# The first expert's rows by counted ranks, and the selection for all experts beside its products

## What is computed

```python
def _ec_moe(h, w_router, w_gate, w_up, w_down):
    Bn, T, _ = h.shape
    cap = EC_CAPACITY_FACTOR * T // N_EXPERTS
    probs = jax.nn.softmax((h @ w_router).astype(jnp.float32), axis=-1)
    gates, idx = lax.top_k(jnp.swapaxes(probs, 1, 2), cap)
    bidx = jnp.arange(Bn)[:, None, None]
    xs = h[bidx, idx]
    a = jax.nn.silu(jnp.einsum('becd,edf->becf', xs, w_gate)) * jnp.einsum('becd,edf->becf', xs, w_up)
    y = jnp.einsum('becf,efd->becd', a, w_down) * gates[..., None].astype(h.dtype)
    return jnp.zeros_like(h).at[bidx, idx].add(y)

# in the layer:   x = x + gate1 * mixer(...);  h = rmsnorm(x) * (1 + scale2) + shift2
#                 x = x + gate2 * _ec_moe(h, ...)
# latent and context tokens each choose within their own set; the order of an expert's rows does not matter
```

## Time and profile before

| | |
|---|---|
| median of 3 runs | 855.3 us (855.23 to 855.87) |
| profiled execution | 855.45 us |
| its span | 853.7 us |
| PE busy | 831.0 us, 97% of the span |
| DVE busy | 493.0 us, 58% |
| ACT busy | 236.8 us, 28% |
| POOL busy | 63.1 us, 7% |
| granted TensorE clock, mean | 0.995 |
| DMA | 275.34 MB, mean 323 GB/s |

### The profile page before, as it was taken

How to read it: one execution, slowest core, us unless ns; L and a number is a source line. 1 busy time by engine, 2 the same in 40 slices (tenths; PEclk the granted TensorE clock), 3 DMA queues, 4 the chain that set the end, 5 groups by cost and what they waited for, 6 DMA issues and landing times.

```text
span 853.7 us, 14512 instructions
## 1 busy us (share of the span) xinstructions
PE 831.0 (97%) x6037; PEld 456.5 (53%) x6037; DVE 493.0 (58%) x1197; ACT 236.8 (28%) x466; POOL 63.1 (7%) x73
## 2 busy tenths in 40 slices
PE   6999999999999998999999999999999999999995
PEld 5798899899898876333333333333333333333322
DVE  3576552859366566576546556456456456465436
ACT  5557544544243335020110110111111011011005
POOL 1000000000000003110010011011011011010033
PEclk9999999999999999999999999999999999999998
DMA  9955625352319938999999999999999999999984
GB/s 329 301 203 189 223 82 197 113 197 78 133 31 344 369 126 319 416 408 428 411 411 428 412 410 430 412 408 429 412 412 422 416 412 419 419 412 412 427 340 161
DMA packets 51045, 275.34 MB, mean 323 GB/s; under 512 B 5226, under 2 KB 14542, under 8 KB 38820
## 3 DMA queue, kind: packets, MB, share of 16 engines
q1 hardware_dynamic: 45484, 255.68, 74.4%
q0 software_dynamic: 3968, 13.83, 5.5%
q10 hardware_dynamic: 1528, 4.90, 1.5%
HBM read 260.90 MB, written 13.57 MB: 321 GB/s over the span
## 4 chain that ended last, share of the span: by engine, by line
PE 88%; DMA 3%; DVE 3%; ACT 2%; SPq 1%; issue 1%; POOL 0%; POOLq 0%; DVEq 0%; ACTq 0%
PE pair L2365 25%; PE pair L1975 16%; PE pair L2387 13%; PE pair L2337 13%; PE pair L2396 7%; PE pair L2212 6%; PE pair L1915 2%; PE pair L2010 2%; DMA scale_b<-in_w_mod 2%; DMA p1w<-in_w_mod 1%; DMA xs<-hn,first_ctx 1%; PE pair L2123 1%; PE pair L1924 1%; PE pair L2145 0%; PE pair L2141 0%
## 5 line engine op out<-in xcount | busy, mean ns | idle before, releaser
L2365 PE MATMUL pair<-ring,xT 128*64 128x512 f32 x1024 | 224.1, 594 | 0.9 <-ACT xT L1124 0.9
L2365 PEld LDWEIGHTS pair<-ring,xT 128*64 128x64 f32 x1024 | 71.9, 137 | 142.9 <-issue 142.3
L2387 PE MATMUL pair<-ring,aT 128*64 128x512 f32 x512 | 113.4, 595 | 0.6 <-DVE aT L1754 0.6
L2337 PE MATMUL pair<-ring,xT 128*32 128x512 f32 x1024 | 113.4, 594 | 0.0
L1132 ACT ACTIVATE xT<-xT,mod,scale 128x64 f32<-128x64 f32 x120 | 41.4, 427 | 217.0 <-DVE xT L1754 201.4
L1754 DVE STREAM_TRANSPOSE xT<-xs 32x256 f32<-32x256 f32 x180 | 78.3, 435 | 3.0
L1754 DVE STREAM_TRANSPOSE aT<-act_l 32x128 f32<-32x128 f32 x256 | 77.5, 303 | 4.1
L2387 PEld LDWEIGHTS pair<-ring,aT 128*64 128x64 f32 x512 | 35.8, 137 | 77.6 <-issue 76.8
L1975 PE MATMUL pair<-hT_hi,w_hi 128*128 128x320 f32 x320 | 76.0, 319 | 0.0
L2337 PEld LDWEIGHTS pair<-ring,xT 128*32 128x32 f32 x1024 | 31.5, 110 | 80.2 <-issue 80.2
L1975 PE MATMUL pair<-hT_lo,w_hi 128*128 128x320 f32 x320 | 73.1, 310 | 0.0
(11 more groups left out here) (305 smaller groups left out, 937.3 us busy)
## 6 DMA issues: line engine op xcount, KB each, us to landing
ring<-in_w_up SPq DMA_DIRECT2D x32, 2048.0 KB, 29.0
ring<-in_w_down SPq DMA_DIRECT2D x32, 2048.0 KB, 18.8
ring<-in_w_gate SPq DMA_DIRECT2D x31, 2048.0 KB, 24.6
p1w<-in_w_mod SPq DMA_DIRECT2D x8, 2048.0 KB, 8.7
p1w<-in_w_in SPq DMA_DIRECT2D x5, 2048.0 KB, 8.0
p1w<-in_w_mod SPq DMA_DIRECT2D x7, 1024.0 KB, 11.4
x_sb<-in_x_sample SPq DMA_DIRECT2D x8, 512.0 KB, 5.7
p1w<-in_w_out SPq DMA_DIRECT2D x2, 2048.0 KB, 8.6
```

What stands on the lines that cost most here:

```text
L2337: ins = mm(ctx_ps[32 * g:32 * g + 32, :], xt[:, 4 * half + j, CAP_L:96], w[:, j, n * 512:(n + 1) * 512], start=half == 0 and j == 0, stop= ...
L2365: ins = mm(ps[64 * n:64 * n + 64, :], xt[:, kk, 0:CAP_L], w[:, j, n * 512:(n + 1) * 512], start=kk == 0, stop=kk == KC - 1)
L2387: ins = mm(y_ps[0][r:r + 64, :], aT[:, j, 64 * fh:64 * fh + 64], wd[:, j, n * 512:(n + 1) * 512], start=fh == 0 and j == 0, stop=fh == 1 a ...
```

## The change

Expert 0's latent rows no longer come from the eight rounds. TensorE spreads expert 0's probabilities of the 512 latent tokens over all partitions (`eR`). For each token VectorE counts how many others have a larger probability (equal ones count if they come earlier), which is its rank (`first_ranks`); a comparison with 0 to 63 gives a one-hot matrix (`first_hot`). TensorE multiplies it with the token numbers and the probabilities (`sel`, `selg`, `choose_first`, in the middle of the context tile's projection), which gives the 64 indices and gains. The eight rounds, the context tile's residual, norm and router, and the context choice are then cut up and stand between one another on VectorE; on TensorE the context router, `pTc`, `ixTc`, `ixT`, the second row of `g2` and `pcT` lie within or behind expert 0's latent products. One half of the context residual moves from ScalarE and GpSimd to VectorE (`ctx_high`), the copy of the context router's parts and the scaled context rows move from ScalarE to VectorE. The fillers are gone. Block 6 of the weights is issued ahead of the wait for `ctx_scaled`.

```diff
             sp.wait_ge(xs_full[0], 16)
+            load_rows(6)
             sp.wait_ge(ctx_scaled, 1)
             sp.dma_start(hn[tile(NT - 1), :], xr[:, 0, :]).then_inc(hn_out[0], 16)
-            load_rows(6)
...
+            pool.wait_ge(job_done, job("lg2") + 1)
+            g.iota(probs_t[:, :, E:E + 1], pattern=[[P, NT], [0, 1]], base=0, channel_multiplier=1,
+                   allow_small_or_imprecise_dtypes=True)
+            g.iota(places[:, :], pattern=[[1, CAP_L]], base=0, channel_multiplier=0, allow_small_or_imprecise_dtypes=True)
+            link(g.memset(lower[:, :], 1.0))
+            g.affine_select(out=lower[:, :], in_=lower[:, :], compare_op=ALU.is_ge, fill=0.0, base=-1,
+                            pattern=[[-1, P]], channel_multiplier=1).then_inc(pad_ready, 1)
...
             gather_first()
+            pool.wait_ge(idx_ready, 4)
             gather(1)
-            pool.wait_ge(idx_ready, 3)
+            pool.wait_ge(idx_ready, 5)
...
+            first_tokens(0, 2)
+            h2_turn(NT - 1)
+            act.wait_ge(x2c_ready, 2)
+            square_sum(NT - 1)
+            first_tokens(2, KC)
+            act.wait_ge(smax_ready, 2)
+            a.activation(probs[:, NT - 1, :], probs[:, NT - 1, :], ACT.Exp).then_inc(exp_ready, 1)
...
+                for t in range(NT - 1):
+                    ins = v.scalar_tensor_tensor(out=compared[4][:, tile(t)], in0=row[:, tile(t)], scalar=probs[:, t, 0:1],
+                                                 in1=lower[:, :], op0=ALU.is_equal, op1=ALU.mult, accum_out=ranks[:, 0, t:t + 1])
+                link(ins)
+                for t in range(1, NT - 1):
+                    ins = v.tensor_scalar(early[t], row[:, 0:P * t], probs[:, t, 0:1], ranks[:, 0, t:t + 1],
+                                          ALU.is_ge, ALU.add, accum_out=ranks[:, 1, t:t + 1])
+                link(ins)
+                for t in range(NT - 1):
+                    link(v.tensor_scalar(late[t], row[:, P * t:T_LAT], probs[:, t, 0:1],
+                                         ranks[:, 1 if t else 0, t:t + 1], ALU.is_gt, ALU.add, accum_out=ranks[:, 2, t:t + 1]))
+                    v.tensor_scalar(first_hot[:, t, :], places[:, :], ranks[:, 2, t:t + 1], None, ALU.is_equal).then_inc(selr_ready, 1)
...
             softmax(0, NT - 1, 1)
-            largest(probs_half[:, :], CAP_L, topv_l, topi_l)
+            normalise(NT - 2)
+            first_ranks()
+            turned_probs()
+            first_chosen()
+            rounds(0, 2)
+            ctx_high()
+            v.memset(xT[:, 0, :, SLOTS:96], 0.0).then_inc(pads_zero, 1)
+            rounds(2, 3)
+            high_chunks(NT - 1)
+            rounds(3, 4)
+            ctx_parts()
+            ctx_normal()
+            router_row(NT - 1)
+            softmax(NT - 1, NT, 2)
+            rounds(4, 5)
+            ctx_largest()
+            rounds(5, 6)
+            pp = result(dve, "ixTc")
+            v.tensor_copy(first_ctx[:, :], pp[0:CAP_C, E:2 * E][:, 0:1]).then_inc(idx_ready, 1)
+            rounds(6, 8)
             merge_halves()
...
                 if k == 0:
+                    choice()
+                    dve.wait_ge(g2_ready, 2)
                     tokens(e + 1, k + 1)
...
+            def first_row():
+                pe.wait_ge(probs_ready, 1)
+                pp = claim(pe, "eR")
+                for t in range(NT - 1):
+                    ins = turn(pp[:, tile(t)], probs[:, t, 0:1].to_broadcast([P, P]), ident[:, :])
+                end(ins, "eR")
+
+            def choose_first():
+                pe.wait_ge(selr_ready, NT - 1)
+                pp = claim(pe, "sel")
+                for half in range(2):
+                    for t in range(NT - 1):
+                        ins = mm(pp[CAP_L * half:CAP_L * half + CAP_L, 0:2], first_hot[:, t, :], probs_t[:, t, 0:E + 1:E],
+                                 start=t == 0, stop=t == NT - 2)
+                    end(ins, ("sel", "selg")[half])
+
+            first_row()
             turn_probs("pT", 1, range(NT - 1))
...
-            output_projection(4, 1)
+            output_projection(4, 1, range(3))
+            choose_first()
+            output_projection(4, 1, range(3, KC))
             pe.wait_ge(mod_ready, 16)
             gate_rows(2, 5 * KC, 0)
-            gate_rows(2, 5 * KC, 1)
-            keep_warm("ixT", 7)
-            turn_indices("ixT", 1)
-            turn_tile(4)
-            keep_warm("lg4", 5)
-            router(4)
...
                             if kk == 1:
+                                router(4)
+                            if kk == 2:
+                                router_sum(4)
+                            if kk == 3:
                                 turn_probs("pTc", 2, (NT - 1,))
-                            if kk == 3:
-                                turn_indices("ixTc", 2)
-                            if kk == KC - 1:
-                                turn_choice()
...
+                            if kk == 5:
+                                turn_indices("ixTc", 1)
...
                 if k == 0:
+                    turn_indices("ixT", 2)
+                    gate_rows(2, 5 * KC, 1)
+                    pe.wait_ge(xT_lat, 1)
+                    pe.wait_ge(xs_ctx, 16)
+                    for c in range(KC):
+                        ins = turn_first_rows(c, slice(CAP_L, SLOTS))
+                    ins.then_inc(xTc_done, 1)
                     claim_last(pe, 1)
-                    claim_last(pe, 3)
                 if not turns:
                     for half in range(2):
                         context_products(half)
+                if k == 0:
+                    turn_choice()
+                    claim_last(pe, 3)
```

More of the change, by code:

```diff
@@ L132, in claims_in_order @@
     names += [n for n in JOBS[JOBS.index("modT0b"):JOBS.index("wo0")] if n not in OPENED and n not in LATE]
-    return names + LATE + [n for n in JOBS[JOBS.index("wo4") + 1:] if n != "lp4"]
+    return names + LATE + [n for n in JOBS[JOBS.index("wo4") + 1:] if n not in UNCLAIMED]
 CLAIMS = claims_in_order()
@@ L156 @@
 LAST_ON = place_jobs()
-assert sorted(CLAIMS + [f"lp{t}" for t in range(NT)]) == sorted(JOBS)
+assert sorted(CLAIMS + UNCLAIMED) == sorted(JOBS)
 QUARTERS = ["0a", "2a", "0b", "2b", "1a", "3a", "1b", "3b"]
@@ L330, in build @@
         RTK = B_YL
-        probs = at("probs", RTK, [P, NT, E])
+        probs_t = at("probs", RTK, [P, NT, E + 1])
+        probs = probs_t[:, :, 0:E]
+        compared = [at(f"compared{k}", W_YT + 2560 * k, [P, T_LAT]) for k in range(5)]
+        ranks = at("ranks", W_YT + 2560 * 5, [P, 3, NT])
+        first_hot = at("first_hot", W_YT + 2560 * 6, [P, NT - 1, CAP_L])
+        lower = at("lower", W_YT + 2560 * 7, [P, P])
+        places = at("places", W_YT + 2560 * 7 + 512, [P, CAP_L])
         probsT = at("probsT", RTK + 512, [E, T])
@@ L669, in _ @@
             pool.wait_ge(g1_ready, 2)
[L670 to L675, removed]
+            cols = slice(0, 512)
+            pool.wait_ge(wo4_read, 1)
+            link(g.tensor_tensor(xr[:, 0, cols], xr[:, 0, cols], gate1b[:, 1, cols], ALU.mult))
+            pool.wait_ge(x_in[NT - 1], 32)
+            g.tensor_tensor(x_sb[:, NT - 1, cols], x_sb[:, NT - 1, cols], xr[:, 0, cols], ALU.add).then_inc(x2c_ready, 1)
             pool.wait_ge(idx_ready, 1)
@@ L1664, in softmax, with first_ranks @@
                                 ).then_inc(probs_ready, 1)
[L1665 to L1676 removed]
+            def first_ranks():
+                row = result(dve, "eR")[:, 0:T_LAT]
+                early = (None, compared[3][:, 0:P], compared[2][:, 0:2 * P], compared[3][:, P:4 * P])
+                late = (compared[1][:, :], compared[0][:, 0:3 * P], compared[2][:, 2 * P:4 * P], compared[0][:, 3 * P:4 * P])
+                dve.wait_ge(pad_ready, 1)
+                for t in range(NT - 1):
[10 more added lines that the diff above has]
+                    v.tensor_scalar(first_hot[:, t, :], places[:, :], ranks[:, 2, t:t + 1], None, ALU.is_equal).then_inc(selr_ready, 1)
@@ new lines, in ctx_largest, with largest @@
+            def ctx_largest():
+                pp = result(dve, "pTc")
+                v.tensor_copy(probsT[:, T_LAT:T], pp[0:E, 0:P]).then_inc(probsT_ready, 1)
+                dve.wait_ge(probsT_ready, 2)
+                largest(probsT[:, T_LAT:T], CAP_C, topv_c, topi_c, 0, CAP_C // 8)
+                v.tensor_scalar(selr[:, 4, CAP_L:SLOTS], topi_c[:, 0:CAP_C], float(T_LAT), None, ALU.add
+                                ).then_inc(selr_ready, 1)
+            def largest(rows, cap, top_v, top_i, lo, hi):
+                for r in range(lo, hi):
@@ L2407, in _ @@
                     ins.then_inc(xTp_done, 1)
+            turn_tile(4)
             claim_last(pe, 0)
```

167 lines of the change are left out of this document (77 added, 90 removed).

## The result

The changed kernel takes 861.04 us (median of 9 runs, 858.77 to 864.28); the kernel before takes 855.66 us beside it (9 runs, 854.09 to 858.12). The ratio is 1.0063, with a 95% interval of 1.0044 to 1.0081. It is slower, by 5.4 us. The forecast was 854.0 us and no measurable difference; the time lies outside the range, on the side that I gave 0.13.

The account below looks back on a forecast made before the run. TensorE, 88% of the chain, was taken as the bound, with the selection ahead of the second expert. That expert would start at 368.45 instead of 369.81, 1.35 us sooner: 855.3 - 1.35 = 853.95, say 854.0 us; range 851.9 to 856.8.

Parts of the forecast that it names:

- the side that I gave 0.13: Whole kernel: slower than 857.0 us, from a long clock fall and missed ranks or waits; chance 0.13.
- The ranks, 5.6 us: VectorE's counting and comparisons for expert 0: 4.5 to 6.5 us, taken as 5.6, from 317.13 to 322.8.
- TensorE waits 0.85 us, which costs nothing yet: TensorE reaches the one-hot products at 322.0 and waits 0.85 us for the ranks, at no cost yet.
- The fillers are gone, off the path: Ahead of expert 0's first product: removing TensorE's filler matmuls, 1.73 us and more, was taken as off the path.
- clock rival: TensorE's clock falls to 1.2 GHz between 346.8 and 350.4; 5 us lose 2.5, giving 856.5 us; chance 0.10.
- Block 6 goes past the context store. At nothing: SyncE's queue: block 6, issued about 328 ahead of the context store, is through in time and costs nothing.
- The context gather, 4.5 us: Gather of the context rows ahead of the context products: takes 4.5 us and lands at 347.8.
- The late rival (6.4): Context gather stays at 6.4 us: second expert starts 0.9 us worse, 854.9 us; chance 0.15.
- one-hot products: 16 small TensorE instructions that give expert 0's indices and gains: 0.6 us for the index, 1.2 for both.
- TensorE's latent products: From 331.2: 13.9 us, plus 1.1 for router, sums and turns, plus 0.4 wait, to 346.8.
- the rigid pattern behind the second expert: From the second expert on, TensorE alone repeats every 31.50 us, so any gain must show as its earlier start.
- the balance of VectorE and TensorE at 350: VectorE has the context tokens ready at 350.35, TensorE's turns are done by then; context products start at 350.4.

Follow-up runs that it names:

- the kernel with GpSimd's pieces late: Changed kernel with GpSimd's two context residual operations moved behind the first gather; 860.10 us, 1.0042 of the kernel before.
- row 6: Changed kernel with the one-hot products behind the sixth, not third, row of the last output projection; 856.32 us, 1.0004 of the kernel before.
- the kernel with the store first: Changed kernel with block 6 of the weights issued behind the context store again; 858.83 us, 1.0031 of the kernel before.
- the repeat: Second measurement, 12 runs, of the changed kernel with one-hot products behind the sixth row and fillers in three TensorE waits; 854.15 us, 0.9995 of the kernel before.
- the stray run at 858.4: One of eleven runs, first measurement of the changed kernel with sixth-row one-hot products and fillers in three TensorE waits; median 854.58 us, ten runs at 853.4 to 855.1.
- the kernel with all waits filled: Changed kernel, one-hot products still behind the third row, fillers in every TensorE wait, block 6 behind the context store; 856.58 us, 1.0011 of the kernel before.

## Why the prediction was wrong, point by point

- **The ranks, 5.6 us: mis-sized, 7.2.** The sum output is a read of 0.08 us, far below the 0.18 taken from ScalarE. But the operations follow each other more slowly than I had it: from the count over 512 columns to the comparison behind it there are 0.86 us (319.46 to 320.32), where its columns and 0.1 fixed make 0.66. Without GpSimd beside them the ranks last 6.0 us, 0.4 above what I took. And two comparisons of 0.13 grew to 0.84. The hold by GpSimd is 1.2 us, by the kernel with GpSimd's pieces late. I had read GpSimd's pieces only for when GpSimd would be free, not for what stands beside them.
- **"TensorE waits 0.85 us, which costs nothing yet": the step that failed.** The wait was 2.37 us, and I had put its consequences at nothing. Behind it nine matmuls ran at a pitch of some 0.43 us for 0.233: about 1.7 us. The projection ended at 330.1 and not at 327.6, VectorE waited 2.53 us for it, and the store went out at 338.54 instead of 336.1. Two experiments bear it out: filled, the first product comes 1.4 us sooner; with the products behind row 6, the store goes out at 335.91.
- **"The fillers are gone, off the path": wrong.** In the kernel before they are worth 4.6 us. I had argued from the 1.29 us wait at 329.72 that such a wait leaves the clock alone. It is 2.89 us without the fillers, and the clock falls; and 1.21 us were enough in the kernel with GpSimd's pieces late. So the length of one wait doesn't tell it. My clock rival was the right mechanism with the right sign. I looked for it only at 346.8 to 350.4; it struck first at 325. It also had 0.10, and priced one fall, where there were two: about 1.7 us and 2.2 us (1.88 at the products, 0.37 at the turns). The Trainium skill's sentence that I named there ("TensorE: Matmul & The Clock Gate", "What's actually happening"), idleness throttles and activity releases, holds in direction: nine matmuls after the first fall the clock was back at its upper level (2.4 GHz).
- **"Block 6 goes past the context store. At nothing": wrong.** The store takes 8.7 us for 4.5 before, and 3.1 with block 6 behind it. It holds the gather of the context rows from 344.8, when its index is ready, until 347.3: 2.5 us. I had block 6 issued at 328 and through by the time of the store. But block 5 waits for the output projection, and block 6 stands behind it on the queue (the gathered rows, for which it waits too, had landed at 329.3), so the late projection sent both out at 330.3 to 330.6 (block 5 went out at 325.16 before), and block 6 was in flight until 344.7. Where the projection ends early (row 6), the store lands after 5.1 us, ahead of the index, and the step is free. I had named the gather as the transfer to watch, and not the store that it waits for.
- **The context gather, 4.5 us:** it took 5.46, and 5.5 to 7.0 in the experiments. The late rival (6.4) was nearer in most of them.
- **The sum.** From forecast to measured start of the second expert (368.45 to 375.38) there are 6.9 us. The first wait makes all behind it late: 1.2 of ranks and 1.6 of clock, less 0.35 for one-hot products that took 0.86 and not 1.2, are 2.45; the store goes out 2.4 late, the context index comes 2.1 late. To these 2.1 the store's landing adds 2.5, the issue 0.2 and the gather 1.0, which is 5.8. Of it 0.95 is taken by the slack that this gather had in the forecast. The second fall of the clock adds 0.37 at the turns and 1.88 at the products: 7.1, within 0.2 of what was measured.
- **A slip in the sum.** The terms of TensorE's latent products (331.2, 13.9, 1.1 and 0.4) make 346.6 and not 346.8; nothing hangs on it.
- **The last 0.8 us.** The span grew by 6.4, the second expert's start by 5.6. At the end VectorE and GpSimd meet as in the kernel with the store first:

```profile
843.93 0.73 DVE L1223 SCALAR_TENSOR_TENSOR rms<-rms 128x3 f32<-128x3 f32 x1
```

```profile
839.93 4.72 POOL L746 TENSOR_TENSOR final_gain<-x_sb,gfin 128x1024 f32<-128x1024 f32 x2 [0.80 <-DMA x_sb<-sums]
```

  0.73 us for 0.16 in the profile of before, ending at 844.66 when GpSimd's piece ends at 844.65, and the chain of waits goes through it: 0.57 of the 0.8. The rest is open.
- **Right:** the rigid pattern behind the second expert; that no weights are late; the order of VectorE's work; the balance of VectorE and TensorE at 350. The kernel with the products behind row 6 has the forecast's numbers: context products at 350.17 (350.4), second expert at 368.20 (368.45), profiled execution 854.2 us (854.0). The chain of the prediction is that of a kernel in which TensorE doesn't wait at 322. Part of the match is luck: that profile is one of the lower group, the median is 856.3, and the longer gather (5.55 us for 4.5) is made up for by an index that is ready 0.5 us sooner and by slack.
- **Not settled:** why a wait of 1.21 us was enough for the fall in the kernel with GpSimd's pieces late, while waits of 2.32 us (row 6) left the clock alone in the profile taken; in which stretch the clock fell in the two stray runs of the repeat; what the stray run at 858.4 is; and what holds the last 1 us of the kernel with all waits filled.

## What to carry to other kernels

Before you take filler matmuls out, or put a wait where they stood, price the wait with the slow clock behind it and ask who waits for the slowed work: here two waits of 2.4 and 3.0 us cost 3.9 us more in the matmuls behind them in the profile, and moving nine matmuls in front of the first wait gave 4.1 of the 5.4 us back. Look at the granted clock of every run, not only of the profiled one: it tells whether a spread of the times is the clock. A store that a gather waits for belongs ahead of a 2 MB load on the same queue only if the gather would otherwise wait for it; where the index is later, leave the load first. Read each engine's timeline against GpSimd's: here a tiny `tensor_scalar` on SBUF, or a `scalar_tensor_tensor` with both inputs in SBUF, that met a running GpSimd `tensor_tensor` lasted until that ended. Other forms did not (below).

## What the runs showed of the hardware that I had not expected

- **A hold, not a slowdown.** A comparison of 64 columns in SBUF took 0.25 us alone and 0.84 beside GpSimd's `tensor_tensor`; an operation on 3 columns with both inputs in SBUF took 0.16 us, and 0.73, 1.30, 1.56 and 1.79 in four kernels. Where I compared the ends, VectorE's lay 0.01 to 0.06 us behind GpSimd's. The counting operations, with an input in PSUM, ran at their own time during the same pieces (0.53 us for 256 columns from 321.97, against 0.54 without GpSimd). Nor were the rounds of the kernel before held, though their input lies in SBUF: a maximum over 256 columns took 0.42 us at 321.70 and at 323.07, inside GpSimd's pieces, and 0.42 at 324.43, outside them.
- **The same 512 KB store** landed after 3.0 to 3.1 us in five of the six profiles with block 6 behind it and 4.5 in the sixth, that of the kernel before (why is open: block 5, ahead of it, had landed); after 5.1 to 6.5 us with block 6 issued 6.7 us ahead of it and block 5 about 3 us ahead of that (four profiles); after 8.6 to 8.8 us with both issued together, 7.7 to 8.3 us ahead (four profiles). Against the 3.1 us, block 6 ahead of it on its queue costs it 2.0 to 3.4 us where it went out 3 us behind block 5, and 5.6 us where both went out together.
- **The clock fell after waits of 1.21 and 2.37 us** amid otherwise full work, though for the longer wait not in every run (above), and the matmuls at the lower level came up to 2.3 us after the wait had ended (pitch 0.43 us from 325.0 on, wait over at 322.68). I had looked for it only inside long idle stretches.
- **The read of VectorE's sum output is an instruction of its own, 0.08 us.** The Trainium skill ("VectorE: DVE Perf Modes", "Two Vector instructions with no wait between them") says that it is one; the trace now shows it, and at a price that made my upper end of 2.0 us for eleven too high by 1.1.
